# Two-block transformer kernel: gate rows moved into the unused rows of the forgetting attention's keys, and the hg head norm moved behind the attention's first blocks

## The reference

```python
def fox_attention(q, k, v, log_f):            # b, 4 heads, 512, 64
    c = jnp.cumsum(log_f, axis=-1)
    ...
        logits = einsum('bhqd,bhkd->bhqk', qi, k) * scale + ci[..., :, None] - c[:, :, None, :]
        logits = jnp.where(pos_k[None, :] <= pos_q[:, None], logits, -jnp.inf)
        probs = jax.nn.softmax(logits, axis=-1)
        return jnp.einsum('bhqk,bhkd->bhqd', probs, v)
...
    o_a = rms_norm(fox_attention(q, k, split_heads(v, FOX_HEADS), log_f), fox_on_g)
    ...
    o_c = rms_norm(o_c, hg_on_g) * jax.nn.silu(split_heads(hg_g, HG_HEADS))
...
        x = x + mixed.astype(x.dtype) @ w_out[l]
```

## Time and profile before

| | us |
|---|---|
| median of 3 runs | 1970.09 (1969.88 to 1970.34) |
| the profiled execution | 1968.11 |
| its span | 1966.3 |
| PE busy | 1900.4 (97%) |
| DVE busy | 996.0 (51%) |
| ACT busy | 749.6 (38%) |
| POOL busy | 231.4 (12%) |

### The profile page before, as it was taken

The page is one execution under the profiler, slowest core; times in us unless marked ns, Lnnn a source line. Parts: engine busy times, 40 slices in busy tenths (PEclk is TensorE's granted clock), DMA queues, the critical chain, the costliest instruction groups (busy, mean ns, idle before and its releaser), DMA issues.

```text
span 1966.3 us, 25391 instructions
## 1 busy us (share of the span) xinstructions
PE 1900.4 (97%) x8897; PEld 1542.0 (78%) x8897; DVE 996.0 (51%) x1467; ACT 749.6 (38%) x1081; POOL 231.4 (12%) x196
## 2 busy tenths in 40 slices
PE   8989978889999999999999999999999999999998
PEld 6778856567788888888888888888876788888887
DVE  6464478754777673344454443433556444444322
ACT  6533543443544443232243323322455443333222
POOL 0051000012111111100021111110000121111100
PEclk9999989899999999999999999999999999999999
DMA  6310200012333333333333333333321133333332
GB/s 190 86 33 1 65 22 22 22 65 59 92 96 96 96 94 98 98 96 97 97 97 96 96 96 96 93 97 99 102 71 43 33 97 96 96 96 95 91 96 72
DMA packets 309221, 161.26 MB, mean 82 GB/s; under 512 B 12688, under 2 KB 306832, under 8 KB 309024
## 3 DMA queue, kind: packets, MB, share of 16 engines
q1 hardware_dynamic: 308080, 157.64, 28.0%
q0 software_dynamic: 640, 2.17, 0.3%
q10 hardware_dynamic: 432, 0.52, 0.1%
HBM read 158.21 MB, written 2.10 MB: 82 GB/s over the span
## 4 chain that ended last, share of the span: by engine, by line
PE 90%; DVE 5%; ACT 2%; issue 2%; DMA 1%; POOL 0%; ACTq 0%; DVEq 0%; POOLq 0%
PE ps L369 26%; PE ps L370 26%; PE ps L371 26%; PE ps L1446 1%; PE ps L1061 1%; PE ps L1652 1%; PE ps L1461 1%; PE ps L1073 1%; PE ps L1942 1%; PE ps L1943 1%; PE ps L934 1%; PE ps L1437 1%; PE ps L1643 1%; ACT whi L356 0%; DVE xlo L443 0%
## 5 line engine op out<-in xcount | busy, mean ns | idle before, releaser
L369 PE MATMUL ps<-xhi,whi 128*128 128x512 f32 x1656 | 660.9, 399 | 3.2 <-ACT ecol L987 2.1
L370 PE MATMUL ps<-xlo,whi 128*128 128x512 f32 x1656 | 646.3, 390 | 0.0
L371 PE MATMUL ps<-xhi,wlo 128*128 128x512 f32 x1656 | 646.3, 390 | 0.0
L356 ACT ACTIVATE whi<-raw 128x1024 fp32r<-128x1024 f32 (+2 forms) x297 | 308.9, 1040 | 707.2 <-PE ps L371 706.6
L364 DVE TENSOR_TENSOR wlo<-raw,whi 128x1024 fp32r<-128x1024 f32 (+2 forms) x297 | 365.6, 1231 | 279.4 <-ACT whi L356 279.3
L369 PEld LDWEIGHTS ps<-xhi,whi 128*128 128x128 f32 x1656 | 312.0, 188 | 72.4 <-issue 8.9
L370 PEld LDWEIGHTS ps<-xlo,whi 128*128 128x128 f32 x1656 | 312.0, 188 | 66.2 <-issue 3.7
L371 PEld LDWEIGHTS ps<-xhi,wlo 128*128 128x128 f32 x1656 | 311.8, 188 | 65.6
L619 DVE TENSOR_TENSOR zS<-ps,rs 128x512 f32<-128x512 f32 x132 | 91.3, 692 | 296.9 <-PE ps L371 284.6
L371 PE MATMUL ps<-h_hi,wlo 128*128 128x512 f32 x528 | 205.4, 389 | 0.0
L369 PE MATMUL ps<-h_hi,whi 128*128 128x512 f32 x528 | 205.4, 389 | 0.0
(11 more groups left out here) (322 smaller groups left out, 1779.2 us busy)
## 6 DMA issues: line engine op xcount, KB each, us to landing
raw<-in_conv_ffn_w SPq DMA_DIRECT2D x52, 512.0 KB, 3.8
raw<-in_mla_ffn_w SPq DMA_DIRECT2D x52, 512.0 KB, 3.8
raw<-in_w_up SPq DMA_DIRECT2D x44, 512.0 KB, 3.8
raw<-in_w_in SPq DMA_DIRECT2D x28, 512.0 KB, 3.8
raw<-in_conv_w_in SPq DMA_DIRECT2D x24, 512.0 KB, 3.8
raw<-in_w_down SPq DMA_DIRECT2D x16, 448.0 KB, 3.6
raw<-in_conv_ffn_w SPq DMA_DIRECT2D x16, 448.0 KB, 3.6
raw<-in_mla_ffn_w SPq DMA_DIRECT2D x16, 448.0 KB, 3.6
```

The lines of the kernel that those rows point to most:

```text
L356: a.activation(whi[:, u % PARTS, 0:n], raw[:, u % RAW, 0:n], ACT.Copy).then_inc(hi_split, 1)
L369: t_.matmul(out, wh, xh, start=first, stop=False)
L370: t_.matmul(out, wh, xl, start=False, stop=False)
L371: return t_.matmul(out, wl, xh, start=False, stop=last)
```

## The change

The second product per block of logits goes. Of each head's k tile the 64 rows of the other head are free: POOL now copies the four gate rows of `grow` there (rows 64 to 67 for the heads 0 and 2, rows 0 to 3 for 1 and 3). The q tile of each head is masked on ACT in place of k on POOL, with a bias that puts a one into exactly the row of this head's gate (`foxpick`): one product gives both terms. Odd heads need their own copies of q and k, made by ACT. The tiles that hold them, the values and the outputs are others. And the hg norm moves: ACT's squares stay, PE's two sums stand ahead of block 4's logits, ACT's four root steps ahead of block 5's exponential, and DVE's norm and gates behind P of block 4.

```diff
@@ constants
-    sizes += [(f"foxrow{h}", P) for h in range(4)] + [(f"gdnrow{h}", P) for h in range(4)]
+    sizes += [("foxpick", 4)] + [(f"gdnrow{h}", P) for h in range(4)]
...
+    put("foxpick", i[:, None] == np.array([64, 1, 66, 3])[None, :])
@@ attn_act
             for n in range(n_all + LAG):
+                if tag == "fox" and n == 5:
+                    for i in range(2):
+                        act_head_rs(act, "hg out", i, 1.0 / DH)
                 if n < n_all:
@@ attn_dve
                     v.tensor_scalar(pm, pm, stat[:, m % 4, 2:3], None, ALU.mult).then_inc(*step("dve", f"{tag} P{m}"))
+                    if tag == "fox" and m == 4:
+                        dve_la_norm(dve, "hg", "hg_on_g", HG_OUT)
+                        for i in range(2):
+                            la_gate(dve, v, "hg", HG_OUT, i, "dve")
@@
-        FZ, FVT, FO = (2, 3, 14, 15), 12, 10
+        FQ, FK, FVT, FO = (6, 11, 7, 13), (0, 14, 1, 15), 2, 4
@@ pe_fox
             def ready(pe, h):
-                pe.wait_ge(*after(f"fox kz{h}"))
+                pe.wait_ge(*after(f"fox q{h}"))
+                pe.wait_ge(*after(f"fox k{h}"))
...
-                if (h, i) == (0, 2):
+                if (h, i) == (1, 0):
                     pe_head_norm(pe, "hg out", range(2))
-                t_.matmul(out, FOX_QK[h // 2][:, i * P:(i + 1) * P], mx[:, FZ[h], 0:W], start=True, stop=False)
-                return t_.matmul(out, C(f"foxrow{h}"), grow[:, 0:W], start=False, stop=True)
+                return t_.matmul(out, mx[:, FQ[h], i * P:(i + 1) * P], mx[:, FK[h], 0:W], start=True, stop=True)
@@ new
+        def act_fox_heads(act):
+
+            pick = C("foxpick")
+            for p in range(2):
+                q = mx[:, FQ[2 * p], :]
+                act.wait_ge(*after(f"fox qk {p}"))
+                for h in (2 * p + 1, 2 * p):
+                    a.activation(mx[:, FQ[h], :], q, ACT.Identity, scale=C("hmask")[:, h % 2:h % 2 + 1],
+                                 bias=pick[:, h:h + 1]).then_inc(*step("act", f"fox q{h}"))
+            for p in range(2):
+                act.wait_ge(*after(f"fox qk {2 + p}"))
+                a.activation(mx[:, FK[2 * p + 1], :], mx[:, FK[2 * p], :], ACT.Copy).then_inc(
+                    *step("act", f"fox k copy{p}"))
@@ pool_fox
-                pool.wait_ge(*after(f"fox qk {2 + h // 2}"))
-                if h == 1:
-                    pool.wait_ge(*after("hg1 intra14 0 full"))
-                g.tensor_scalar(mx[:, FZ[h], :], FOX_QK[2 + h // 2], C("hmask")[:, h % 2:h % 2 + 1], None,
-                                ALU.mult).then_inc(*step("pool", f"fox kz{h}"))
+                rows = slice(64, 68) if h % 2 == 0 else slice(0, 4)
+                pool.wait_ge(*after(f"fox k copy{h // 2}"))
+                g.tensor_copy(mx[rows, FK[h], :], grow[0:4, :]).then_inc(*step("pool", f"fox k{h}"))
@@ the engines' programs
             act_fox_unit(act, 4)
+            act_fox_heads(act)
             act_fox_unit(act, 5)
             act_fox_v(act)
-            act_la_out(act, "hg", HG_OUT)
+            for i, (o, ready, _) in enumerate(HG_OUT):
+                act.wait_ge(*after(ready))
+                a.activation(sq[:, i, :], o, ACT.Square).then_inc(*step("act", f"hg out square{i}"))
             act_fox(act)
...
             dve_la(dve, "hg1", in_hg1)
-            dve_la_norm(dve, "hg", "hg_on_g", HG_OUT)
-            for i in range(2):
-                la_gate(dve, v, "hg", HG_OUT, i, "dve")
             dve_fox(dve)
```

More of the change, by code:

```diff
@@ L81, in constants @@
     put("perm", (s // 64 == r // 64) & (s % 64 == (r + 32) % 64))
+    put("foxpick", i[:, None] == np.array([64, 1, 66, 3])[None, :])
     for h in range(4):
-        put(f"foxrow{h}", (s == h) & (r >= 0))
         put(f"gdnrow{h}", (s == 64 + h) & (r >= 0))
```

## The result

In the runs on record for both kernels the median went from 1970.28 us to 1973.08 us; the ratio of the changed kernel to the one before is 1.0015, with a 95% interval of 1.0009 to 1.0021. So the change costs about 3.0 us (1.8 to 4.1). The forecast was 1974.3 in a range of 1971.0 to 1977.0. A second group of runs, with both kernels in turn on one chip, gave 1.0017 (1.0008 to 1.0026). One execution of the changed kernel (2746.77 us at a granted clock of 0.65) and one of a later experiment (3176.4 us at 0.56) are slow ones and are left out of the ratios.

A forecast was written before the change was run, and what follows sets the result against it. From PE's first logits to w_out, the gates' end sets the reload of x, for which PE waits. Later reload +3.9, products -2.4, half clock +2.7 make +4.2; with 1968.11 profiled and 2.0 to the median, 1974.3 us, range 1971.0 to 1977.0.

The forecast's parts named there:

- later end of the gates against before: DVE's gates, now behind P4, were to end at 417.98, 3.9 us later than before (bounds 3.4 and 4.4).
- second products behind the reload: From head 2 on, five removed second products on the chain were to save 2.4 us (bounds 1.3 and 4.3).
- half clock behind the wait: PE's work from 427.9 on was to start at half clock, costing 2.7 us (bounds 1.7 and 3.4).
- The front: At the first half's attention, DVE's first mask was to come at 406.47, 7.5 us earlier, and ACT's roots begin at 413.41.
- The reload: From the gates to x's landing 9.70 us as before, 0.24 more to PE; transposes start at 427.9, 3.9 us later.
- a landing less than 9 us behind the gates: Sign named for the forecast being wrong: the reload of x landing sooner behind DVE's gates than 9 us.
- The wait: PE was to stand still for 11 us, from near 416.5, ahead of the reload's transposes, in place of some 1.4.
- The base: Forecast's starting time: the profiled execution of the kernel before, 1968.11 us, with 2.0 added up to the median of 1970.09.
- rivals, 1: PE idles for the reload but comes back at full speed, so the clock costs nothing: +1.5 us, 1971.6; chance 0.13.
- Rival 2: The reload is no longer what PE waits for at head 2: -4.1 us, 1966.0; chance 0.06.
- Rival 3: A second fall of the clock near 445, ahead of w_out: 1.7 to 3 us more, +6.4, 1976.5; chance 0.15.
- Rival 4: The removed second products of heads 2 and 3 pay in full, all 4.3 us: +2.3, 1972.4; chance 0.10.

The follow-up runs named there:

- e9: Changed kernel with three of the reload's four DMAs issued before the gates and six matmuls of unused result in PE's wait; 1965.74 us, ratio 0.9980 to before.
- e3: Changed kernel with eleven matmuls of unused result put in front of the reload's transposes; 1971.41 us, ratio 1.0010 to before.
- after_again: The changed kernel itself, unchanged, timed again as the reference of a second group; 1973.19 us, ratio 1.0017 to before.
- e11: Changed kernel with the hg norm earlier (sums ahead of block 3's logits, gates behind P of block 1), reload in one piece; 1969.65 us, ratio 0.9999 to before.
- e4: Changed kernel, but PE transposes the reloaded x first ahead of head 3, not head 2; 1969.98 us, ratio 0.9996 to before.
- e1: Changed kernel with the hg norm back in front, keeping one product per block; 1967.74 us, ratio 0.9994 to before.
- e2: Kernel before with only the hg norm moved behind P of block 4, two products per block kept; 1975.59 us, ratio 1.0030 to before.
- e5: Changed kernel with the reload's first three DMAs issued once their tiles are free, only the fourth behind the gates; 1966.10 us, ratio 0.9981 to before.
- e7: Changed kernel with three reload DMAs issued early and the reloaded x transposed first ahead of head 3; 1969.69 us, ratio 0.9999 to before.
- e8: Changed kernel with the hg norm back in front, one product per block, and three reload DMAs issued early; 1966.84 us, ratio 0.9985 to before.
- e10: Changed kernel with three reload DMAs issued early and the hg norm's gates earlier, behind P of block 1; 1967.27 us, ratio 0.9989 to before.
- e12: Kernel before with only the reload split, three of its four DMAs issued early; 1969.73 us, ratio 1.0003 to before.

## Why the prediction was right

Point by point, in us from the first logits where nothing else is said:

| step | predicted | measured |
|---|---|---|
| operands on ACT and POOL | hidden, 0 | hidden, 0; POOL 2.96 in place of 7.3 |
| first mask of DVE | 0.7 | 0.73 |
| later end of the gates against before | +3.9 | +3.77 |
| gates to PE's transposes, 9.94 before | 9.94 | 8.54 |
| second products behind the reload | -2.4 | -2.2 (e9) |
| half clock behind the wait | +2.7 | +2.8 (changed kernel over e9; 2.7 over e3 up to head 3) |
| sum in the stage | +4.2 | +2.94 |

**The front** came as worked out: block 3's exponential 4.31 us behind the first mask (4.46 predicted), and the roots begin 2.48 behind that and take 2.60 (2.48 and 2.59 predicted). **The reload** is the term that was off: I let it take what it took in the trace of before, and it took 1.40 us less. The last tile landed 8.3 us behind the gates (422.10 + 6.07 = 428.17), and "a landing less than 9 us behind the gates" was one of the signs that I had named for being wrong; it came, and it says that this term was mis-sized, not that the wait was absent. The same queue needed 9.50 us in after_again (419.23 to 428.73) and 8.54 in the first profile. With 9.50 the sum would be 3.9, near the forecast. Whether the change itself shortens the reload is open. Its last DMA took 7.5 us before and in e11, 7.0 in after_again and e4, 6.2 in e1 and 6.1 in the changed kernel, e2 and e3. The two of 7.5 have DVE at work beside it, but so has e1 with 6.2, and after_again has DVE idle for most of it and 7.0. **The wait** was 9.9 and 10.9 us, for 11 predicted. **The clock** fell as predicted and for 5.6 us of work, between the 4.8 and 6.0 of the earlier trace rows. That it did so is not a rule: behind the same wait it took 4.7 us of work in after_again, 4.1 in e2 and 3.0 in e5. **The base** of the forecast was no typical execution: the profile of before (1968.11) is faster than all 20 executions of the comparison (lowest 1969.05), and the sum carried the 2.0 us up to the median along without a reason. The changed kernel's profile (1973.07) lies at its median, and its transposes of v begin 2.02 us later; so the spans differ by 5.0 us and the medians by 2.8.

Of the rivals, 1 is refuted (half clock in both profiles, and e3 moves when it goes). Rival 2 can't come about with the reload behind the gates. In e4 and e7 PE no longer waits for the reload, and they gain at most 0.8 us on before by their ratios, and not the 4.1 that I had given it; their clock falls at two other places. e5's 3.7 is near that figure by chance, since its reload still landed 4.3 us behind the gates and PE waited 5.88 us for it. Rival 3 did not show in the first profile, but did in after_again, e1, e3, e8, e10 and e11, always between 445 and 458, where head 3's last blocks wait for DVE and ACT; it costs 1.7 us in after_again and in e3, at the low end of the 1.7 to 3 that I had given it. Rival 4 is refuted: the products gave 2.2 us behind the reload in e9, not 4.3. What the forecast did not see is how easily the clock falls: it took the gap of 2.49 us as harmless, on one profile's word.

The chance for slower by over 0.2% was 0.53 and for within 0.42; the measured 0.15% is within, so the likelier side did not come. The 1.4 us of the shorter reload make that difference. The mechanism, the wait and its half clock, came as worked out.

## What to carry to other kernels

An instruction that frees memory for a transfer belongs to the critical path of the transfer, even if its own result is not needed for long; before such an instruction is moved back, count from its end to the first reader of the transfer. Split a transfer by what each part waits for: three quarters of this one waited for the gates without need, and e5, one edit in POOL's queue, turned the loss of 3.3 us into a gain of 3.7. The same edit gave the kernel before nothing (e12): what a split is worth depends on how long the reader waits for the transfer. And where PE's work is thinned in a stage with gaps, price the fall of its clock as well: in the profiles it took back about half of the expected gain in e1 (1.4 of 2.8 us) and all that the products gave in the changed kernel (2.8 against 2.2).

## What the runs showed of the hardware that was not expected

The granted clock in a gap of about 2.5 us fell in one profile and held in another with the same queue on PE. In the gaps of 3.29 us and more shown in this document it fell each time. Fourteen profiles, whose queues on PE and DVE are the same up to the transposes of v, reach these between 403.5 and 406.3. These 2.8 us follow no edit (the changed kernel itself is at 405.8 and 405.2, the three with two products per block at 403.8, 404.4 and 406.0) and are as large as the effects measured here, so profiles were compared from there on and not by their spans. A copy on POOL of 4 rows by 512 took 0.74 us, where a masked copy of 128 rows by 512 took 1.8.
